# The order of two projections in the tail of the differential attention: the sticks' first queries and keys in front of their values

## The reference

```python
h = rms_norm(x, g_pre)
p = h @ w_in                       # 12 parts of 512 columns, and 8 more for the forget gate
qa, ka, va, ga, qs, ks, vs, gs, qf, kf, vf, gf, ff = split(p)
ya = diff_attention(rope(qa), rope(ka), va, lam) * silu(ga)      # 4 heads, two softmaxes each
yb = stick_breaking_attention(qs, ks, vs) * silu(gs)             # 8 heads of 64, "sb"
yc = forgetting_attention(qf, kf, vf, cumsum(log_sigmoid(ff))) * silu(gf)   # 8 heads of 64, "fox"
x = x + rms_norm(concat([ya, yb, yc]) @ w_out, g_post)
```

## Time and profile before

| what | us |
|---|---|
| median of 3 runs | 1973.49 |
| lowest and highest of them | 1972.63, 1975.47 |
| the profiled execution's own time | 1973.32 |
| its span, first to last instruction | 1971.5 |
| PE busy | 1888.8 |
| DVE busy | 779.6 |
| ACT busy | 876.6 |
| POOL busy | 662.5 |

### The profile page before, as it was taken

How to read it: one execution, slowest core, us unless ns; L and a number is a source line. 1 busy time by engine, 2 the same in 40 slices (tenths; PEclk the granted TensorE clock), 3 DMA queues, 4 the chain that set the end, 5 groups by cost and what they waited for, 6 DMA issues and landing times.

```text
span 1971.5 us, 24056 instructions
## 1 busy us (share of the span) xinstructions
PE 1888.8 (96%) x9233; PEld 1539.2 (78%) x9239; DVE 779.6 (40%) x1346; ACT 876.6 (44%) x1727; POOL 662.5 (34%) x278
## 2 busy tenths in 40 slices
PE   7998999899999899989899999999999999999998
PEld 6887787777788678777677888888788878888886
DVE  3435656535444465644645752011350441111002
ACT  4555565544445546555434723333443353233222
POOL 2432233123242233222223544334104424443442
PEclk9999999999999999999999999999999999999999
DMA  4321222212331122211332222222102423222222
GB/s 155 107 64 54 86 75 86 65 51 107 115 111 66 49 80 86 86 54 54 118 128 75 97 97 88 94 86 96 44 1 88 141 73 99 98 100 97 97 97 85
DMA packets 48411, 170.06 MB, mean 86 GB/s; under 512 B 6960, under 2 KB 7216, under 8 KB 47664
## 3 DMA queue, kind: packets, MB, share of 16 engines
q1 hardware_dynamic: 46480, 154.95, 23.9%
q10 hardware_dynamic: 1824, 13.63, 1.8%
HBM read 155.97 MB, written 6.29 MB: 82 GB/s over the span
## 4 chain that ended last, share of the span: by engine, by line
PE 83%; DVE 10%; ACT 4%; issue 3%; DMA 0%; POOL 0%; DVEq 0%; ACTq 0%; POOLq 0%
PE bank L670 13%; PE bank L672 13%; PE bank L671 13%; PE bank L673 10%; PE bank L675 10%; PE bank L674 10%; PE bank L797 2%; PE bank L814 2%; PE bank L775 1%; PE bank L773 1%; PE bank L776 1%; DVE y_tok L1423 1%; PE bank L761 1%; PE bank L828 1%; PE bank L827 1%
## 5 line engine op out<-in xcount | busy, mean ns | idle before, releaser
L653 POOL TENSOR_TENSOR w_hl<-w_raw,w_hl 128x1024 fp32r<-128x1024 f32 x274 | 662.3, 2421 | 1284.6 <-ACT w_hl L925 1284.1
L925 ACT ACTIVATE w_hl<-w_raw 128x1024 fp32r<-128x1024 f32 x274 | 287.7, 1058 | 346.8 <-DMA w_raw<-wstream 346.0
L670 PE MATMUL bank<-act_hl,w_hl 128*128 128x512 f32 x1056 | 427.0, 404 | 3.1 <-DVE act_hl L1296 1.9
L672 PE MATMUL bank<-act_hl,w_hl 128*128 128x512 f32 x1056 | 414.6, 393 | 0.0
L671 PE MATMUL bank<-act_hl,w_hl 128*128 128x512 f32 x1056 | 413.9, 392 | 0.0
L673 PE MATMUL bank<-w_hl,act_hl 128*128 128x512 f32 x672 | 265.8, 396 | 4.7 <-POOL w_hl L653 2.3
L675 PE MATMUL bank<-w_hl,act_hl 128*128 128x512 f32 x672 | 262.4, 390 | 0.0
L674 PE MATMUL bank<-w_hl,act_hl 128*128 128x512 f32 x672 | 262.2, 390 | 0.0
L670 PEld LDWEIGHTS bank<-act_hl,w_hl 128*128 128x128 f32 x1056 | 200.4, 190 | 45.3 <-issue 3.9
L672 PEld LDWEIGHTS bank<-act_hl,w_hl 128*128 128x128 f32 x1056 | 199.8, 189 | 43.4
L671 PEld LDWEIGHTS bank<-act_hl,w_hl 128*128 128x128 f32 x1056 | 200.4, 190 | 40.7 <-issue 2.2
(11 more groups left out here) (231 smaller groups left out, 2798.8 us busy)
## 6 DMA issues: line engine op xcount, KB each, us to landing
w_raw<-wstream SPq DMA_DIRECT2D x274, 512.0 KB, 3.4
q_dup<-q_dup SPq DMA_DIRECT2D x48, 128.0 KB, 3.7
x_spill<-x_res ACTq DMA_DIRECT2D x2, 2048.0 KB, 6.9
x_res<-x_spill ACTq DMA_DIRECT2D x2, 2048.0 KB, 8.3
x_res<-x SPq DMA_DIRECT2D x4, 512.0 KB, 6.4
g_post<-post_gains ACTq DMA_DIRECT2D x4, 512.0 KB, 3.7
x_res<-x ACTq DMA_DIRECT2D x1, 2048.0 KB, 8.4
out<-x_res SPq DMA_DIRECT2D x4, 512.0 KB, 2.6
```

The lines of the kernel that those rows point to most:

```text
L653: nc.gpsimd.tensor_tensor(w_hl[:, slot, 1].rearrange("p c n -> p (c n)"), w_raw[:, slot, :], w_hl[:, slot, 0].rearrange("p c n -> p (c n)" ...
L670: pe.matmul(out_ap, wh, ah, start=start, stop=False)
L672: return pe.matmul(out_ap, wl, ah, start=False, stop=stop)
L925: nc.scalar.activation(w_hl[:, b % RING, 0].rearrange("p c n -> p (c n)"), w_raw[:, b % RING, :], ACT.Copy).then_inc(s_high_done, 1)
```

## The change

In the differential attention the two projections change places: the sticks' q and k (m = 0) are now woven in behind the gates, up to step 10, and their values up to the end. All blocks, drains and DMAs stay; the weights lie in the stream in the new order.

```diff
             if ki == 0:
-                parts = [(project("g", l, 0) + project("v", l, 1), done)]
+                parts = [(project("g", l, 0) + project("qk", l, 1, 0), done)]
 ...
             if more:
-                ahead = project("qk", l, ki + 1, 0)
+                ahead = project("v", l, 1) if ki == 0 else project("qk", l, ki + 1, 0)
             parts.append((ahead + (project("v", l, 2) if ki == 1 else []), 2 * ATT_STEPS[kind]) + (() if more else (True,)))
```

## The result

| | before | after |
|---|---|---|
| median, us (13 runs each) | 1975.06 | 1978.83 |
| lowest and highest | 1972.63, 1976.28 | 1975.25, 1980.55 |
| ratio to before, 95% interval | | 1.0020, 1.0012 to 1.0028 |
| profiled execution: time, span | 1973.32, 1971.5 | 1978.69, 1976.9 |

The change costs 3.77 us, 0.19%: just inside the 0.2% that I took as the edge, and its interval lies wholly on the slow side. The forecast was 1977.0, which was 3.6 us above the profiled execution of before. The absolute number came out 1.8 us higher, and most of that is the kernel before itself, whose median over 13 runs is 1.57 us above that of the 3 runs I had.

A forecast was written before the change was run, and what follows sets the result against it. PE's own list was taken to bound the kernel (busy 1888.8 us, 96% of the span). 1973.32 + 2 x (2.96 - 1.44 + 0.3) gave 1977.0 us, range 1973.8 to 1980.0.

The forecast's parts named there:

- Part 1, the middle drain: In front of step 9 of diff: q and k's longer drain delays step 10's chain, 2.96 us lost per layer.
- Part 2, the end of diff: At the end of diff: the shorter values drain removes three PE waits, 1.44 us won per layer.
- The upper bound of 1.44: At the end of diff: at most 1.44 us won per layer, no other PE wait within 80 us being shortenable.
- Part 3, the clock: Between the stops around step 10 of diff: PE work may run at the low clock, 0.3 us lost per layer.
- The first rival: Around step 10's stops: clock stays low for a further spell, 1.65 us more per layer, 1980.3 us; chance 0.18.
- The sign of 2.0 us more from the first scores of diff to those of sb: In the profile after, both layers: this stretch is longer by 2.0 us (3.0 less the 0.95).
- That the middle drain is covered: At step 9: unseen DVE slack hides the longer drain, only the gain at diff's end acts, 1970.4 us; chance 0.10.
- Faster: Around step 10: DVE slack hides the longer drain and the clock doesn't drop where it did before, 1967.1 us; chance 0.04.
- That it cancels by a gain at step 13: Middle loss at 2.4 us per layer, no clock effect, one half caught by step 13's chain: 1974.0 us; chance 0.07.

The follow-up runs named there:

- halved_values: Kernel before, with the sticks' values drain in front of step 9 of diff cut into two halves of 64 partitions; 1981.08 us, ratio 1.0026.
- light_qk: Kernel after, with the sticks' q and k drain left half undone (only the first head of each pair copied and split); 1968.89 us, ratio 0.9964.
- the fills: Small matmuls on constants put in PE's stops in diff, in the kernel before (1967.96 us, ratio 0.9968) and the kernel after (1969.93 us, ratio 0.9973).
- pull_after: Kernel after, with one half block moved in front of the head turns of steps 10 and 13 of diff, both layers; 1966.21 us, ratio 0.9954.

## Why the prediction was right

**Part 1, the middle drain: right.** 2.96 us per layer was the term, 3.03 is measured (A), and the two stops are 1.37 and 1.55 us, for 1.3 and 1.7. `halved_values` shows that it is the length of the drain: the order of before, with a drain of that length, has A late by 3.01 and 3.05 us and the same two stops.

**Part 2, the end of diff: the mechanism right, the term too small.** All three waits went, and nothing took their place, but they gave 2.21 us per layer and not 1.44. I had added up the idle times of the rows, 0.95 + 0.19 + 0.30. An idle time in these rows counts from the modelled end of the last matmul, while the next one could have started before that end: matmuls of 512 columns are 0.39 us long in the rows and start every 0.23 us. Start to start, the first wait was worth 1.54 - 0.36 = 1.18 us, the second 0.40, the third 0.49, and the block behind the first ran 0.11 faster without waits for banks. This is shown by the markers in four traces (before, after, `light_qk`, `halved_values`). The upper bound of 1.44 in the prediction was therefore no bound.

**Part 3, the clock: too small in the sum, and not explained.** I had allowed 0.3 us per layer, on the argument that before already paid the spell in both layers. With the clock held up the change costs 1.8 us (F with the fills) or 1.64 (the markers), without that 3.77, so about 1 us per layer is left for the clock in the medians; by the interval of the result it can be 0.3 to 1.9. In the one pair of traces it is 2.5, because the two profiled executions lie far apart: that of before, from which I took all my spells, lost 4 us less to the low level than the mean, and that of after 2.4 us more. The first rival had 1.95 us per layer. What it named, the clock kept down longer by a broken stretch, is seen in the trace of after (6.8 and 10.2 us behind step 10's stops), and `pull_after` has a spell in each layer from those stops alone. But the spells at step 13 also grew, behind a stop that didn't change, and `halved_values`, with the same broken stretch, ran at the mean clock of before. So that the broken stretch is what lowers the clock on average is not shown. The sign of 2.0 us more from the first scores of diff to those of sb was not met in the pair of traces, which have 4.4 and 4.2 us; without the clock it is 3.03 - 1.29 = 1.7.

**The sum.** Forecast +5.92 - 2.88 + 0.60 = +3.64; measured +6.06 - 4.42 = +1.64 by the markers, and 2.1 of the 3.77 us between the medians is left for the clock. That last term is the remainder and no measurement of its own. The gain was forecast 1.5 us too small and the clock's cost 1.5 us too small; they have opposite signs and nearly cancel. The direction and the middle drain were understood; that the total came within 0.13 us of the forecast difference is luck.

**The other rivals.** That the middle drain is covered: no, A is 3.03 us late. Faster: no. That it cancels by a gain at step 13: no, the stop there stays at 3.4 us.

What stays open is what sets the number of low spells: `light_qk`'s diff has 10.2 us of low clock in the first layer and 6.8 in the second with the waits of before, which had 3.4 and 6.8, and yet its executions ran at the higher clock in the mean.

## What to carry to other kernels

Where attention chains and dense blocks share the small engines, it isn't enough to ask where a drain's result is needed next. Ask what is queued behind the drain on VectorE: in front of a step whose chain ends in a wait of TensorE, every microsecond of it is passed on, here 3.03 for 3.03. A wait that can't be shortened can be covered: half a block moved in front of each of two head turns per layer gave 12 us, three times what the order of the projections could change. And cost a removed wait from start to start of the matmuls round it, not by the idle time in its row.

## What the runs showed of the hardware

The granted clock fell to its low level of 1.2 GHz at two stops as short as 1.36 and 1.56 us, with half a microsecond of small matmuls between (`pull_after`, once in each layer), for 3.4 us, and cost 1.6 us each time, about as much as the second stop. The Trainium skill ("TensorE: Matmul & The Clock Gate", section "Why this matters for your kernels") warns of idle gaps between bursts of matmuls that are longer than either of these two; the measurement decides, and here the shorter ones sufficed. A stop of 3.42 us in the first layer of before was followed by no fall. Small matmuls on constants in the stops kept the clock at its full level in both layers of both kernels and were worth 7.1 and 8.9 us. Copies and subtractions of 512 columns over 64 partitions took as long as over 128 (0.69 us on DVE, 0.59 and 0.60 us on ACT), so cutting them in halves doubled the drain.
